# A decoder layer whose expert tiles are re-ordered and whose token rows are placed differently in each tile

## What is computed

```python
x = x + concat([o_a, o_b, o_c]) @ w_out
h = rmsnorm(x, norm_ffn)
grp = argmax(h @ w_grp + b_grp)                      # one of 4 groups
top_val, top_idx = top_k(expert_logits[grp], 2)      # two of its 8 experts
w_top = softmax(top_val) * softmax(group_logits)[grp]
for e in range(32):
    a, u = h @ w_e_gate[e], h @ w_e_up[e]            # 1024 x 256 each
    out = out + (silu(a) * u * gate[:, e:e + 1]) @ w_e_down[e]   # 256 x 1024
x = x + out
return rmsnorm(x, norm_final)
```

## Time and profile before

| | us |
|---|---|
| median of 3 runs (lowest, highest) | 1226.47 (1221.49, 1229.13) |
| the profiled execution | 1224.38 |
| its span, first to last instruction | 1222.6 |

### The profile page before, as it was taken

The page is one execution under the profiler, slowest core; times in us unless marked ns, Lnnn a source line. Parts: engine busy times, 40 slices in busy tenths (PEclk is TensorE's granted clock), DMA queues, the critical chain, the costliest instruction groups (busy, mean ns, idle before and its releaser), DMA issues.

```text
span 1222.6 us, 29632 instructions
## 1 busy us (share of the span) xinstructions
PE 1112.5 (91%) x12106; PEld 907.2 (74%) x12106; DVE 581.6 (48%) x1582; ACT 384.1 (31%) x693; POOL 242.2 (20%) x476
## 2 busy tenths in 40 slices
PE   6999899999999999999998999959998999898980
PEld 5989788777887888888777788857676767676750
DVE  5331344225666667665785434484342333333334
ACT  6411112222555555544776222201111111111113
POOL 1020000000432323221573000012222212121210
PEclk9999899999999999999999999959999999899995
DMA  9021754362756755653331544289999999999627
GB/s 352 18 86 39 271 157 144 136 192 89 168 131 182 195 115 135 138 130 86 100 81 40 185 138 136 80 316 360 358 360 340 336 342 331 314 338 340 238 53 276
DMA packets 62021, 239.14 MB, mean 196 GB/s; under 512 B 23328, under 2 KB 24128, under 8 KB 52032
## 3 DMA queue, kind: packets, MB, share of 16 engines
q1 hardware_dynamic: 54272, 220.45, 54.4%
q0 software_dynamic: 7616, 16.80, 5.8%
HBM read 201.14 MB, written 45.88 MB: 202 GB/s over the span
## 4 chain that ended last, share of the span: by engine, by line
PE 64%; DMA 23%; DVE 5%; issue 4%; SPq 2%; ACT 2%; POOL 1%; DVEq 0%; POOLq 0%; ACTq 0%
DMA wdn<-in_wdn 18%; PE PS L1866 12%; PE PS L2044 9%; PE PS L2126 7%; PE PS L2199 7%; PE PS L1855 5%; PE PS L2022 4%; PE PS L2207 4%; PE PS L1983 4%; PE PS L2023 3%; DMA wst<-in_wt 1%; DMA k<-T_d 1%; PE PS L1901 1%; PE PS L2190 1%; PE PS L2016 1%
## 5 line engine op out<-in xcount | busy, mean ns | idle before, releaser
L2199 PEld LDWEIGHTS PS<-XT,wgu 128*64 128x64 f32 x4352 | 192.0, 143 | 52.0 <-issue 50.8
L2199 PE MATMUL PS<-XT,wgu 128*64 128x96 f32 x4352 | 198.8, 254 | 25.2 <-DMA wdn<-in_wdn 14.7
L1118 ACT ACTIVATE pt<-PS,cst 128x512 f32<-128x512 f32 (+3 forms) x288 | 167.2, 650 | 107.3 <-PE PS L2023 82.9
L1425 DVE CUSTOM_DVE_ANT_0 junkm<-PS,cst 128x512 f32<-128x512 f32 (+3 forms) x276 | 133.5, 531 | 78.4 <-PE PS L1983 76.3
L2044 PEld LDWEIGHTS PS<-V,pt 128*64 128x64 f32 x3840 | 121.9, 138 | 22.6 <-issue 11.3
L2044 PE MATMUL PS<-V,pt 128*64 128x65 f32 x3840 | 137.6, 225 | 0.4 <-issue 0.4
L2207 PE MATMUL PS<-wdn,aT 128*96 128x512 f32 x272 | 124.4, 599 | 3.1 <-issue 2.2
L1866 PE MATMUL PS<-hTh,wth 128*128 128x512 f32 x256 | 102.9, 402 | 4.8 <-DVE wtl L1272 4.8
L1754 DVE TENSOR_SCALAR ge<-PS 128x192 f32<-128x192 f32 x34 | 12.2, 358 | 186.6 <-PE PS L2199 186.6
L1866 PE MATMUL PS<-hTl,wth 128*128 128x512 f32 x256 | 100.7, 393 | 0.0
L1866 PE MATMUL PS<-hTh,wtl 128*128 128x512 f32 x256 | 100.7, 393 | 0.0
(11 more groups left out here) (280 smaller groups left out, 1676.2 us busy)
## 6 DMA issues: line engine op xcount, KB each, us to landing
wgu<-in_wgu SPq DMA_DIRECT2D x34, 2048.0 KB, 17.2
wdn<-in_wdn SPq DMA_DIRECT2D x34, 1024.0 KB, 41.0
q<-T_d SPq DMA_DIRECT2D x58, 256.0 KB, 4.3
k<-T_d SPq DMA_DIRECT2D x58, 256.0 KB, 5.5
wst<-in_wt SPq DMA_DIRECT2D x16, 512.0 KB, 6.5
T_d<-thi SPq DMA_DIRECT2D x16, 512.0 KB, 2.6
T_d<-tlo SPq DMA_DIRECT2D x16, 512.0 KB, 3.9
xt<-in_x SPq DMA_DIRECT2D x8, 512.0 KB, 11.6
```

The costliest lines, as they stand in the source:

```text
L1118: ins = nc.scalar.activation(pt[:, (n + 2) % 6, 0:nt * P], PS[:, n % 3, 0:nt * P], ACT.Exp, scale=C("slopes", h, h + 1), bias=C("kb", w, w ...
L1425: V_.tensor_tensor_reduce(out=junk_[:, 0:L], in0=PS[:, bank, 0:L], in1=tab, scale=1.0, scalar=-3e38, op0=ALU.add, op1=ALU.max, accum_out=m ...
L2199: ins = mm(PS[h * HD:(h + 1) * HD, 2 + p, f * CAP:(f + 1) * CAP], wgu[q][:, c, lo:lo + HD], XT[:, p, c, :], start=(c == 0 and f == 0), sto ...
```

## The change

- `EXPERT` becomes `TILE`: the two overflow tiles stand at places 16 and 25 of the order rather than at the end. Scatters that wait for the one before them are then those of tiles 16, 17, 25 and 26.
- `iota` and `rows` hold, for place r, the rank `r // 6 + 16 * (r % 6)` in place of r. Rank k then stands at place `6 * (k % 16) + k // 16`.
- SP loads `wdn[0]` and tile 1 inside the loop's last trip, ahead of the last `h2_store` (line 710), and tile 2 right behind that store, without waiting for the gather of tile 0.
- SP's one loop over tiles 6 to 33 reads the expert number of an overflow tile before it waits for the buffer.
- SP no longer waits for the last down product ahead of its 19 trips; the wait is inside the skipped body.

```diff
-EXPERT = tuple(NE // 4 * (n % 4) + n // 4 for n in range(NE))
+ORDER = [NE // 4 * (n % 4) + n // 4 for n in range(NE)]
+TILE = (*ORDER[:16], NE, *ORDER[16:24], NE + 1, *ORDER[24:])
@@ SP
                 x2_store(t)
+                if t + 1 == NT:
+                    sp_.wait_ge(g_mm, 2 * NT)
+                    sp_.dma_start(wdn[0][:], a["wdn"][0].rearrange("p (k n) -> p k n", k=2)).then_inc(we_in[0], 16)
+                    load_expert(TILE[1], 1)
                 h2_store(t, p)
 
-            sp_.wait_ge(g_mm, 16)
-            sp_.dma_start(wdn[0][:], a["wdn"][0].rearrange("p (k n) -> p k n", k=2)).then_inc(we_in[0], 16)
-            load_expert(EXPERT[1], 1)
+            load_expert(TILE[2], 2)
             sp_.wait_ge(xg_in[0], 16)
-            load_expert(EXPERT[2], 2)
             sp_.wait_ge(h_lg, 8)
-            load_expert(EXPERT[3], 3)
+            load_expert(TILE[3], 3)
             sp_.wait_ge(x2_st, 16 * NT)
             sp_.wait_ge(pe_did, PEV.of("wrow"))
-            load_expert(EXPERT[4], 4)
+            load_expert(TILE[4], 4)
             sp_.wait_ge(dve_did, DV.of("wrow_ov"))
-            load_expert(EXPERT[5], 5)
+            load_expert(TILE[5], 5)
             sp_.dma_start(gfin[:], a["g_fin"]).then_inc(gfin_in, 16)
-            for n in range(RING, NE):
+            for n in range(RING, NB):
+                e = TILE[n]
+                if e >= NE:
+                    e = sp_.value_load(info[0:1, 1 + e - NE:2 + e - NE], min_val=0, max_val=NE - 1)
                 sp_.wait_ge(m_dn, n - RING + 1)
-                load_expert(EXPERT[n], n % RING)
-            for n in range(NE, NB):
-                eid = sp_.value_load(info[0:1, 1 + n - NE:2 + n - NE], min_val=0, max_val=NE - 1)
-                sp_.wait_ge(m_dn, n - RING + 1)
-                load_expert(eid, n % RING)
-            sp_.wait_ge(m_dn, NB)
+                load_expert(e, n % RING)
             n_ovf = sp_.value_load(info[0:1, 0:1], min_val=0, max_val=MAX_OVF - SURE)
             with sp_.Fori(0, MAX_OVF - SURE) as j:
                 with sp_.If(j < n_ovf):
                     eid = sp_.value_load(info[0:1, bass.ds(j + 1 + SURE, 1)], min_val=0, max_val=NE - 1)
+                    sp_.wait_ge(m_dn, NB)
                     sp_.wait_ge(ovf_y, j + 1)
@@ POOL, gather (scatter, and m_out of ACT and DVE: the same for col and n == NE)
-                col = EXPERT[n] if n < NE else n
+                col = TILE[n]
                 pool.wait_ge(m_tr, n + 1)
-                if n == NE:
+                if TILE[n] == NE:
                     pool.wait_ge(dve_did, DV.of("ids_ov"))
@@ POOL, scatter
-                if n >= NE:
+                if TILE[n] >= NE or TILE[n - 1] >= NE:
                     pool.wait_ge(y_st[1 - p], 16 * ((n + 1) // 2))
@@ constants
-    put("iota", np.arange(CAP))
+    rank = np.arange(CAP) // 6 + 16 * (np.arange(CAP) % 6)
+    put("iota", rank)
     put("ocol", NE + np.arange(OCOLS))
-    put("rows", np.arange(CAP) - (CAP - 1) / 2)
+    put("rows", rank - (CAP - 1) / 2)
```

## The result

| | before | changed |
|---|---|---|
| median (lowest, highest) | 1226.40 (1221.49, 1229.13) | 1193.35 (1192.31, 1195.89) |
| the profiled execution | 1224.38 | 1194.30 |
| its span | 1222.6 | 1192.6 |

The ratio of the changed kernel to the one before is 0.9738, with a 95% interval of 0.9702 to 0.9773: 33 us faster, inside the range that was given, and 6 us above the 1187 that was called likeliest. Two single executions that took more than twice as long as their neighbours, 3761.64 us for the kernel with ACT's and DVE's trips early and 2765.27 for the kernel before, are in no median or ratio of this document.

A forecast was written before the change was run, and what follows sets the result against it. Weight loads at 11.21 us a tile, held up on the engines carrying token rows, were taken to bound the kernel, and PE after the change. Span 1222.6 - 35.6 - 3.0 = 1184.0, given as 1187 us median; range 1180 to 1201.

The forecast's parts named there:

- Part 1: Ranks spread over the places: PE needs no wait for weights, and the up product of tile 33 comes 35.6 us sooner.
- the bound of 10.6: The pace of loads, in us a tile, under which the buffers hold out and PE never waits.
- price of a row: 0.62 us for each row gathered and scattered on an engine, on top of 7.51 us of weights a tile.
- forecast of 10.2: Pace of the transfers with spread ranks, in us a tile: 7.51 of weights plus 4.3 rows at 0.62.
- 9.68 x 32: PE's time without waits from the up product of tile 1 to that of tile 33, 828.07 to 1137.8.
- Part 2: First weights, of tiles 1 and 2, requested earlier: 0 us in the end, 7.5 if Part 1 did nothing.
- Part 3: Overflow tiles in the middle of the order: some scatters come late, but PE does not wait; cost 0.
- Rival E: Waits of scatters 16, 17, 25 and 26 reach PE: slower, from a landing of 22.8 us on; chance 0.03.
- Part 4: SP's 19 trips run before the end: loads of `xf` start 3.5 us sooner, the end comes 3.0 us sooner.
- B: No change: the engines' total binds, so the pace stays 11.21 us a tile; 1216 us, chance 0.09.
- C: Faster, but rows cost more on full engines: pace 11.0 us a tile, 11 us late, 1198 us; chance 0.05.
- D: No change: some engine that had few rows is slow with indexed rows; pace 12.0, 1226 us, chance 0.03.

The follow-up runs named there:

- thin kernels: The changed kernel with half of each up product left out, once with ranks spread and once packed: 1178.56 and 1202.58 us, one execution each.
- light kernel: The changed kernel, loading only a quarter of `wgu` and half of `wdn` from tile 6 on: 1186.25 us, ratio 0.969.

## Why the prediction held, and where it was off

**Part 1, right in mechanism.** The uneven backlog and the six neighbouring places to an engine were read from the earlier trace rows; the landings 30 and 5 us apart and the paces of 11.0 to 11.1 and 10.2 to 10.3 bear them out. PE never waited for a load, as the bound of 10.6 said. The price of a row is not borne out. At 0.62 us, the 1.7 rows between 6 and 4.3 make 1.05 us of pace; the thin kernels differ by 0.79 to 0.85. An estimate from these is 0.46 to 0.50 a row, on 8.1 to 8.2 for the weights rather than 7.51. The forecast of 10.2 held because the lower price and the higher base cancel at 4.3 rows. No run took the rows away, so neither number is shown. It decides nothing here, as PE sets the time.

**Part 1, the term that was mis-sized: 9.68 x 32.** It took a tile without holes for the mean tile. The chain of before had holes of this kind too, of 0.45, 1.70, 1.38 and 0.79 us, each ending 1.3 to 1.4 us after a packet of PE's program. The first two stand at the places of the changed kernel's first two, in tiles 5 and 6, the others in down products, at other places. The prediction has no term for them, only "small gaps". What PE waited for before, from 838 to 1174, names 8.4 us of "issue" beside the 14.7 for `wdn`:

```profile
PE PS L2199 <- issue: 6.0, 4, 2.1
PE PS L2207 <- issue: 2.2, 2, 1.4
```

With the wait for `wdn` gone the holes are on the path that sets the end. In the changed kernel eight up products are longer than 5.43, by 0.82, 1.19, 0.23, 1.36, 0.52, 1.39, 1.05 and 1.63, in all 8.2 us; that is the 8.1 of the table. The waits list 6.2 of them; the other 2 are in the products beside the holes, which took longer. The mean tile is 317.9 / 32 = 9.93, and with it the sum would have been 1192 for the span against the 1192.6 measured.

**Part 2, called 0, cost 0.7.** The prediction let the gather take 1 to 2 us more, all of it hidden by DVE's half of `XT`. It took 3.2 more (7.89 against 4.70), and the 2.73 of "issue" ahead of the first up product did not cover that. By the rule of the Trainium skill that was cited there, DMA: Bandwidth & Descriptors, section Queues, rings and completion order, the estimate was 3.8 and a slip of 1: nearer than what was preferred to it. The weights were not through by 810; the engines still moved 438 GB/s from 811 to 812. The prediction named a first up product after 817 as a sign that part 2 was wrong, and it came at 818.18. Of that 0.9 is the later g, but counted from g it is still 10.24 us where 9.93 was the bound. So this step failed: a cost that was put at 0. It was small beside the rest.

**Part 3, right at 0.** POOL did wait for scatters that had not landed, at the four that the change names, and the lateness was passed on from one to the next: scatter 16 came 2.6 us late and scatter 17 4.7, where 2.2 and 4.4 had been said (engine, line, what it waited for: us, times, longest; then two scatters in time order, with the idle time before them):

```profile
POOL x_d L919 <- DMA x_d<-YO,ids: 17.3, 3, 5.9
...
1001.90 1.44 POOL L919 DMA_INDIRECT x_d<-YO,ids  x1 [5.89 <-DMA x_d<-YO,ids]
1013.75 1.44 POOL L919 DMA_INDIRECT x_d<-YO,ids  x1 [8.06 <-PE PS L2191]
```

The three waits are those of scatters 16, 25 and 26; the 8.06 of scatter 17 is put down to PE by the view, though it too follows the start of the scatter before it by 11.85 us, the time of a landing. Scatter 18, at 1018.68, is on time again, and PE waited for none of it. Rival E needed 14.2 us of landing for a wait of PE. But the part also brought nothing: with the overflow tiles last the end of the span came no later after T.

**Part 4, -3.0 predicted, -4.0 measured.** The first square came at T + 11.31 where T + 11.3 had been said, and for the reason given, ACT's own trips; their last move, in the changed kernel, is at T + 11.0:

```profile
L1207 ACTq MOVE  x20: 29/29/38, 1164.0 to 1172.0; - x20
```

`xf` was loaded from T + 5.9 rather than T + 7.1, as the last scatter was through 4.2 us after its issue rather than 5.4, and the squares after the first, which waited for data before, did not wait: the work behind the first square took 20.2 us against 21.7. The prediction had allowed for up to 3.5.

**Signs and rivals.** The chain stayed on PE, the clock at 1.0, and no `YO` waited for a scatter near 1000 or 1080. That the two loads of a tile land a few us apart is shown by the thin spread kernel alone (5 us); the profile of the changed kernel gives no landings for them. B's size was near for the case in which part 1 did nothing (1216 said, 1212 measured with packed ranks), and its mechanism was wrong. C would have needed a pace of 11.0. D and E are answered above.

## What to carry to other kernels

When two landings of one queue lie far apart, look for the engines whose backlog is longer. Here an indexed transfer with a fixed table of 96 places and 60 real rows loaded only the engines of the used places, and spreading the real rows over the table cost nothing. When a sum makes an engine the new bound, take its time per step from many steps with all their small gaps in, not from a clean one: gaps that a larger wait covered come out when that wait goes. And ask of every further edit to the same kernel whether the bound still lies there; of four parts here one brought 27 us by itself and 18 on top of the others, one 3, and two nothing that the runs could tell.

## What the runs showed of the hardware that was not expected

- PE's instructions are fetched through the same DMA engines as the data. With 340 GB/s of weights and rows (838 to 1150) PE loses 8.1 us in 32 tiles to it, with light loads (149 GB/s) 0.0. The holes come in pairs or with a longer product beside them, at tiles 5 and 6, 12 and 13, 20 and 21, 27 and 28, though about one packet is fetched in each tile. The packets' starts show the same rhythm: in each group of eight or nine all but the last four packets start at most 30 products later in the program than in the light kernel, the last four 42 to 103 later, and the holes follow the last two. The Trainium skill, Runtime: NRT & Kernel Launch, section Instruction fetch mechanics, has PE's instruction memory at 2,048 instructions, filled in blocks of 16 KB. With 144 products and 144 weight loads that would be 7.1 tiles, near the 7 and 8 between the pairs, which is an estimate. No run tried whether that is why; it stays open.
- A gather of a few dozen rows takes 7.89 us while weights are in flight and 4.70 to 4.85 with idle engines.
- Filling the first ten or the last ten blocks of places gives the same time within 3 us: none of the last six blocks was found slower for rows than the first six.
